# 64 bytes of padding ahead of the residual stream in SBUF: a whole network in float32 on one core

## The chip, the core and the metric

The kernel runs on one core of one Trainium2 chip. The metric is the time of one execution on the device, in microseconds (us), from the first to the last instruction with what lies around it. Less is better.

## What is computed

A batch of one, 512 tokens of width 1024, in float32, through a chain of blocks; the matrices stream in from HBM.

```python
# first block: HGRN2 mixer (8 heads, both directions, 256 context tokens), then a mixture of experts
h = modulate(x, norm1_g, sh1, sc1);   x = x + g1 * hgrn2_mixer(h, h_ctx, ...)
h2 = modulate(x, norm2_g, sh2, sc2);  x = x + g2 * moe_ffn(h2)   # 16 experts in 4 groups, top 2 of one group
x = rms_norm(x, final_g)
# second block, twice (mixer 0: differential attention + RWKV-7; mixer 1: retention)
for i in range(2):
    x = x + 0.5 * rms_norm(swiglu(rms_norm(x, g[0]), ffn_wgu[i, 0], ffn_wd[i, 0]), g[1])
    x = x + rms_norm(mixer_i(rms_norm(x, g[2])), g[3])
    x = x + 0.5 * rms_norm(swiglu(rms_norm(x, g[4]), ffn_wgu[i, 1], ffn_wd[i, 1]), g[5])
```

`swiglu(x) = (silu(x @ w_gate) * (x @ w_up)) @ w_down` has a hidden width of 2816, an expert one of 256.

## The kernel before

**Precision.** TensorE takes float32 products in a short form (`float32r`) of one pass. A value `v` is therefore kept as two tiles, `v_hi` (the short form) and `v_lo` (the rest), and a product is three matmuls into one bank: weights hi with data hi, weights hi with data lo, weights lo with data hi (`pe_products`, L353 to L355). In `matmul(out, a, b)`, `a` is the stationary operand (the weights that the array holds) and `b` is streamed; the profile writes the streamed one first, so that `bank<-mix_hi,sum_hi` streams `mix_hi` against weights in `sum_hi`. Matmuls on plain float32 tiles (transposes, small products of the mixers) take two passes.

**Weights.** A weight block is 128 x 1024 in float32, 512 KB, 4096 bytes a partition. SP issues their loads in order into a ring of four slots, `raw`; ACT copies a block into `whi` and DVE subtracts into `wlo` (L325 and L344; in the MoE stage L309 and L337). The MoE stage has a ring of eight: block `m` goes to `raw`, `whi`, `wlo` where `m % 8 < 4` and to `raw2`, `whi2`, `wlo2` else (`moe_raw`, `moe_hi`, `moe_lo`). In the profile the buffer numbers are left out, so both read `raw`, `whi`, `wlo`.

**MoE stage.** Here the weights are streamed and the tokens are stationary: per item (7 token tiles x 4 experts) 24 matmuls of 512 columns for gate and up (L2812 to L2814: `xs_hi`, `xs_lo` stationary), and 12 for down (L2840 to L2842: `at_hi`, `at_lo`). Item `i` takes blocks `6i - 2` to `6i + 1` for gate and up, so item 11 (from 685.50 us) begins with four blocks from `whi` and item 13 (from 703.52 us) has four from `whi2`. Between the first and the second block of an item lie the transposes of the item before (L2824).

**Mixer input.** The context's 256 columns, hi and lo side by side, are `hc` (`[P, 8, 512]`); `pe_block` streams them whole against `whi` (L379, L377) and their hi half against `wlo` (L380, L376).

**Seven-product passes.** Two of the three passes of an FFN's gate and up (8 pairs of blocks each) use seven half-size products in place of eight, Strassen's way. `pe_seven_pass` issues per pair the products 11, s1, 22 (of the pair before), s2, s4, 12, s3, of 12 matmuls with 256 columns each (`pe_product`, L961 to L963). Products 11 and 12 stream `h` against `whi`/`wlo`; s1 and s4 stream `h` against sums of weight blocks, `sum_hi`/`sum_lo`; 22 and s3 stream sums of `h`, `mix_hi`/`mix_lo`, against `whi`/`wlo`; s2 streams `mix` against `sum`. DVE makes the sums (L1080 to L1110), ACT their hi parts (L1024, L1033).

**Layout.** SBUF is laid out by hand, in bytes a partition. In `build`, `bump` puts a tensor at `at` and moves on by its size, rounded up to 64; `base` is the first free byte rounded up to 64, 16512 here, which is 129 x 128. In front of `x` stand `raw` to `shift2`, together 124608 bytes, an odd multiple of 64, so that `x` begins at 141120, 64 bytes past a multiple of 128. `k.low` is where `x` begins, `k.top` the end of `a32`; the stages lay their own tensors over `x` and what is behind it, from `k.low`, from `k.top` or from the place of `acc`, `sq` or `a32`: `hc`, `z_st`, `keep`, `cum` and the mixer's others (from `k.low`), `x1`, `xc1`, `whi2` (at `acc`), `raw2`, `hrow` and `wlo2` (from `k.top`), `sums`, `sum_hi`, `sum_lo`, `mix_hi`, `mix_lo` (behind half of `a32`), the retention's `r_v`, `r_qk`, `r_gate`, `r_y`, and the RWKV tensors from `rkv` (at `acc`) on. The hi and lo parts of `h` and `a`, and what is laid over them (`xs_hi`, `xs_lo`, `xrow`, `at_hi`, `ytok`, the first `held` blocks, `q_a`, `kv_a`), stand in front of `x`. All these tensors are plain rows: a tile's address in a partition is its tensor's plus a multiple of 512 bytes in the matmuls that the prediction speaks of.

Of the kernel before, what the change touches and what calls it, by code (L numbers as in the profile page):

```python
# [4783 lines left out]
def build(nc, W, vecs, small, xT, out, phases):  # L4784
    k = Kernel()
# [4 lines left out]
    with ExitStack() as ctx:  # L4790
# [10 lines left out]
        at = 0  # L4801
        def bump(name, shape, dt=F32):
            nonlocal at
            size = int(np.prod(shape[1:])) * (1 if dt == I8 else 4)
            t = sb(name, shape, dt, at=at)
            at += -(-size // 64) * 64
            return t
# [23 lines left out]
        k.shift1 = bump("shift1", [P, 2, DC])  # L4831
        k.gain2 = bump("gain2", [P, DC])
        k.shift2 = bump("shift2", [P, DC])
        k.low = at
        k.x = bump("x", [P, DC, T])
        k.acc = bump("acc", [P, DC, T])
        k.sq = bump("sq", [P, 2, T])
# [256 lines left out]
```

## Time and profile before

| | |
|---|---|
| median of three runs | 3105.99 us (3100.77 to 3107.02) |
| profiled execution: span, first to last instruction | 3101.5 us |
| profiled execution's own time | not given beside its span |
| instructions | 49298 |
| PE busy | 3016.2 us, 97%, 19037 matmuls |
| DVE busy | 2130.9 us, 69% |
| ACT busy | 1528.4 us, 49% |
| mean rate of DMA | 114 GB/s over the span |
| granted TensorE clock, mean | 0.990 |

Matmuls are pipelined: one starts before the one ahead has ended, and their ends are modelled. What a matmul takes of PE's time is therefore the distance from its start to the next one's start, which the timeline gives; the mean duration of a group is longer. The stages stand in this order: mixer input and HGRN2 mixer to about 549 us, MoE to 840, FFN to about 1300, attention and RWKV to 1700, two FFNs, retention from about 2300, and the last FFN.

### The profile page before, as it was taken

To read this page: it belongs to the slowest core of one execution; us is meant where nothing else is said; L and a number is where in the kernel's file an instruction comes from. 1 tells how busy PE (TensorE), PEld (TensorE's weight loads), DVE (VectorE), ACT (ScalarE), POOL (GpSimd) and SP (SyncE) were. 2 spreads that over 40 slices of the span, in tenths; PEclk is the share of its full clock that TensorE was granted. 3 is DMA by queue.
4 is the path that set the end of the run, shared out by engine and by line. 5 is a ranking of instruction groups with operands and counts; after the bars stand their busy time and mean duration, and the time that the engine had idled before them with its cause. 6 is when DMAs were issued, how large, how long until landed. Compare 5 with 4: busy or idle time off the path is not lost.

```text
span 3101.5 us, 49298 instructions
## 1 busy us (share of the span) xinstructions
PE 3016.2 (97%) x19037; PEld 2555.3 (82%) x19037; DVE 2130.9 (69%) x3065; ACT 1528.4 (49%) x2263; POOL 65.0 (2%) x115
## 2 busy tenths in 40 slices
PE   7999999899999999998999999999999999999997
PEld 3888887688779898667878989789988787778996
DVE  5576666899878586775468857786764443588685
ACT  4454645677745354563245535454443332455452
POOL 1000000000000000300000000000000000000000
PEclk9999999899999999999999999999999999999999
DMA  5222222799823332110023232233232222223221
GB/s 226 89 75 76 80 81 83 268 373 379 336 68 109 109 107 89 62 62 19 17 68 102 107 104 102 84 114 109 102 103 82 76 85 78 80 76 123 102 102 68
DMA packets 97101, 354.81 MB, mean 114 GB/s; under 512 B 10896, under 2 KB 11280, under 8 KB 96528
## 3 DMA queue, kind: packets, MB, share of 16 engines
q1 hardware_dynamic: 92448, 334.54, 30.5%
q0 software_dynamic: 3168, 11.54, 1.0%
q10 hardware_dynamic: 1296, 6.11, 0.5%
q8 instruction: 132, 2.16, 0.3%
q14 instruction: 57, 0.47, 0.0%
HBM read 344.27 MB, written 7.86 MB: 114 GB/s over the span
## 4 chain that ended last, share of the span: by engine, by line
PE 89%; DVE 5%; ACT 4%; issue 1%; DMA 1%; POOL 0%; SPq 0%; ACTq 0%; DVEq 0%; POOLq 0%
PE bank L353 13%; PE bank L355 13%; PE bank L354 13%; PE bank L961 7%; PE bank L963 7%; PE bank L962 7%; PE bank L2812 2%; PE bank L2814 2%; PE bank L2813 2%; PE bank L557 2%; PE bank L558 1%; PE bank L562 1%; PE cbank L379 1%; PE bank L3969 1%; PE gbank L1646 1%
## 5 line engine op out<-in xcount | busy, mean ns | idle before, releaser
L325 ACT ACTIVATE whi<-raw 128x1024 fp32r<-128x1024 f32 x310 | 319.3, 1051 | 219.1 <-PE bank L355 182.3
L344 DVE TENSOR_TENSOR wlo<-raw,whi 128x1024 fp32r<-128x1024 f32 x310 | 375.6, 1222 | 70.3 <-ACT whi L325 69.3
L353 PE MATMUL bank<-h_hi_buf,whi 128*128 128x512 f32 x1008 | 410.1, 407 | 8.1 <-DVE h_lo_buf L493 5.1
L355 PE MATMUL bank<-h_hi_buf,wlo 128*128 128x512 f32 x1008 | 394.6, 391 | 0.0
L354 PE MATMUL bank<-h_lo_buf,whi 128*128 128x512 f32 x1008 | 394.2, 391 | 0.0
L353 PE MATMUL bank<-a_hi_buf,whi 128*128 128x512 f32 x832 | 324.9, 390 | 0.5 <-DVE wlo L344 0.5
L354 PE MATMUL bank<-a_lo_buf,whi 128*128 128x512 f32 x832 | 323.7, 389 | 0.0
L355 PE MATMUL bank<-a_hi_buf,wlo 128*128 128x512 f32 x832 | 323.7, 389 | 0.0
L353 PEld LDWEIGHTS bank<-h_hi_buf,whi 128*128 128x128 f32 x1008 | 190.1, 189 | 54.6 <-DVE h_lo_buf L493 6.8
L355 PEld LDWEIGHTS bank<-h_hi_buf,wlo 128*128 128x128 f32 x1008 | 190.0, 188 | 41.3
L354 PEld LDWEIGHTS bank<-h_lo_buf,whi 128*128 128x128 f32 x1008 | 190.4, 189 | 40.2 <-issue 4.1
L337 DVE TENSOR_TENSOR wlo<-raw,whi 128x1024 fp32r<-128x1024 f32 x168 | 196.6, 1219 | 11.7 <-ACT whi L309 11.6
L353 PEld LDWEIGHTS bank<-a_hi_buf,whi 128*128 128x128 f32 x832 | 156.1, 188 | 33.5 <-DVE wlo L344 0.9
L355 PEld LDWEIGHTS bank<-a_hi_buf,wlo 128*128 128x128 f32 x832 | 156.2, 188 | 32.5
L354 PEld LDWEIGHTS bank<-a_lo_buf,whi 128*128 128x128 f32 x832 | 156.2, 188 | 32.1 <-issue 0.2
L1004 ACT ACTIVATE snap<-bank 128x256 f32<-128x256 f32 x256 | 96.6, 377 | 167.9 <-PE bank L963 167.9
L309 ACT ACTIVATE whi<-raw 128x1024 fp32r<-128x1024 f32 x168 | 168.0, 1055 | 12.9 <-DMA raw<-in_w 8.3
L1102 DVE TENSOR_TENSOR wlo<-raw,whi 128x1536 fp32r<-128x1536 f32 x64 | 112.6, 1759 | 52.3 <-ACT whi L1024 51.9
L961 PE MATMUL bank<-mix_hi,whi 128*128 128x256 f32 x512 | 144.2, 282 | 3.8 <-ACT snap L1004 3.8
L963 PE MATMUL bank<-h_hi_buf,wlo 128*128 128x256 f32 x512 | 144.6, 282 | 0.0
L961 PE MATMUL bank<-h_hi_buf,whi 128*128 128x256 f32 x512 | 144.2, 282 | 0.0
L962 PE MATMUL bank<-h_lo_buf,whi 128*128 128x256 f32 x512 | 144.0, 281 | 0.0
(724 smaller groups left out, 7229.1 us busy)
## 6 DMA issues: line engine op xcount, KB each, us to landing
raw<-in_w SPq DMA_DIRECT2D x622, 512.0 KB, 4.0
held<-in_w SPq DMA_DIRECT2D x12, 512.0 KB, 16.5
x<-in_x ACTq DMA_DIRECT2D x2, 2048.0 KB, 11.2
sorted_y<-ysb POOLq DMA_DIRECT2D x6, 512.0 KB, 7.6
token_rows<-hrow POOLq DMA_DIRECT2D x4, 512.0 KB, 4.2
out<-x SPq DMA_DIRECT2D x8, 256.0 KB, 2.0
xc<-in_xc ACTq DMA_DIRECT2D x1, 1024.0 KB, 8.7
sorted_y<-zrow POOLq DMA_DIRECT2D x1, 512.0 KB, 3.1
```

What stands on the lines that cost most here:

```text
L309: act.activation(moe_hi(k, m), moe_raw(k, m), ACT.Copy).then_inc(k.split_hi, 1)
L325: act.activation(weights(k, g)[0], k.raw[:, g.slot, :], ACT.Copy).then_inc(k.split_hi, 2 * RING + 1 if first == COND_GROUPS * RING else 1)
L337: dve.tensor_tensor(moe_lo(k, m), moe_raw(k, m), moe_hi(k, m).bitcast(F32), ALU.subtract).then_inc(k.split_lo, 1)
L344: dve.tensor_tensor(lo, k.raw[:, g.slot, :], hi.bitcast(F32), ALU.subtract).then_inc(k.split_lo, 2 * RING + 1 if first == COND_GROUPS * RI ...
L353: pe.matmul(out, w_hi, hi, start=(t == 0), stop=False)
L354: pe.matmul(out, w_hi, lo, start=False, stop=False)
L355: return pe.matmul(out, w_lo, hi, start=False, stop=(t == tiles - 1))
L961: pe.matmul(out, w_hi[:, w], m_hi, start=(fresh and t == 0), stop=False, skip_group_check=True)
L962: pe.matmul(out, w_hi[:, w], m_lo, start=False, stop=False, skip_group_check=True)
L963: last = pe.matmul(out, w_lo[:, w], m_hi, start=False, stop=(t == HALF_K - 1), skip_group_check=True)
L1004: act.activation(dst, k.bank[bank % RING][:, cols], ACT.Copy).then_inc(k.snapped, 1)
L1102: dve.tensor_tensor(pair_view(k.wlo, g)[:, T:], pair_view(k.raw, g)[:, T:], pair_view(k.whi, g)[:, T:].bitcast(F32), ALU.subtract).then_in ...
```

## The change

`k.low`, and `at` with it, is rounded up to a multiple of 128 before `x` is placed. Since `base` is a multiple of 128 too, every address from `x` on grows by 64 bytes.

```diff
         k.shift1 = bump("shift1", [P, 2, DC])
         k.gain2 = bump("gain2", [P, DC])
         k.shift2 = bump("shift2", [P, DC])
-        k.low = at
+        k.low = at = -(-at // 128) * 128
         k.x = bump("x", [P, DC, T])
         k.acc = bump("acc", [P, DC, T])
         k.sq = bump("sq", [P, 2, T])
```

| tensor | address before | after | remainder by 128 |
|---|---|---|---|
| `raw`, `whi`, `wlo` | 16512, 32896, 49280 | the same | 0 |
| `h_hi_buf`, `h_lo_buf` | 65664, 82048 | the same | 0 |
| `xs_hi`, `at_hi` | 65664, 90240 | the same | 0 |
| `a_hi_buf`, `a_lo_buf` | 98432, 114816 | the same | 0 |
| `ident` | 137856 | the same | 0 |
| `x`, `hc` | 141120 | 141184 | 64 to 0 |
| `acc`, `whi2` | 157504 | 157568 | 64 to 0 |
| `sums` | 184128 | 184192 | 64 to 0 |
| `wlo2`, `sum_hi` | 186176, 192320 | 186240, 192384 | 64 to 0 |
| `raw2`, `mix_hi` | 202560, 204608 | 202624, 204672 | 64 to 0 |
| `mat_at`, `inv`, `inv_t` | 210304, 212352, 214400 | 64 more | 0 to 64 |
| `e_neg`, `kkr`, `tmp1`, `tmp2` | 216480, 218528, 220576, 222624 | 64 more | 32 to 96 |

The instructions of every engine, their order, their waits and the transfers are the same in both kernels.

## Rows read from the trace of the kernel before

**Rows 1.** The page: busy time, share of the span, instructions; the chain by engine
```profile
PE 3016.2 (97%) x19037; PEld 2555.3 (82%) x19037; DVE 2130.9 (69%) x3065; ACT 1528.4 (49%) x2263; POOL 65.0 (2%) x115
...
PE 89%; DVE 5%; ACT 4%; issue 1%; DMA 1%; POOL 0%; SPq 0%; ACTq 0%; DVEq 0%; POOLq 0%
```

**Rows 2.** Groups by shape on DVE and ACT: count | busy us, mean ns | idle before
```profile
L1102 DVE TENSOR_TENSOR wlo<-raw,whi 128x1536 fp32r<-128x1536 f32 x64 | 112.6, 1759 | 52.3 <-ACT whi L1024 51.9
L1110 DVE TENSOR_TENSOR sum_lo<-sums,sum_hi 128x1536 fp32r<-128x1536 f32 x64 | 111.9, 1749 | 6.9 <-ACT sum_hi L1033 6.9
...
L1033 ACT ACTIVATE sum_hi<-sums 128x1536 fp32r<-128x1536 f32 x64 | 95.3, 1488 | 33.4 <-PE bank L963 33.4
L1024 ACT ACTIVATE whi<-raw 128x1536 fp32r<-128x1536 f32 x64 | 95.1, 1486 | 43.2 <-PE bank L963 43.2
```

**Rows 3.** Windows view, 1102 to 1142 us, within a seven-product pass
```profile
core 0: us, PE busy (x) PEld busy (x) DVE busy (x) ACT busy (x) POOL busy (x), PEclk, DMA share, GB/s
1102.00:1142.00 40.00, 40.00 (x343) 40.00 (x342) 35.55 (x46) 23.84 (x36) 0.00 (x0) 1.00 0.31 110
```

**Rows 4.** Timeline of PE, first matmul of each product: start us, duration us, instruction
```profile
1102.67 0.28 PE L961 MATMUL bank<-h_hi_buf,whi 128*128 128x256 f32 x1
...
1104.10 0.28 PE L961 MATMUL bank<-h_hi_buf,sum_hi 128*128 128x256 f32 x1
...
1105.45 0.28 PE L961 MATMUL bank<-mix_hi,whi 128*128 128x256 f32 x1
...
1106.87 0.28 PE L961 MATMUL bank<-mix_hi,sum_hi 128*128 128x256 f32 x1
...
1108.31 0.28 PE L961 MATMUL bank<-h_hi_buf,sum_hi 128*128 128x256 f32 x1
...
1109.73 0.28 PE L961 MATMUL bank<-h_hi_buf,whi 128*128 128x256 f32 x1
...
1111.16 0.29 PE L961 MATMUL bank<-mix_hi,whi 128*128 128x256 f32 x1
...
1112.54 0.28 PE L961 MATMUL bank<-h_hi_buf,whi 128*128 128x256 f32 x1
```

**Rows 5.** Groups by shape on PE
```profile
L353 PE MATMUL bank<-a_hi_buf,whi 128*128 128x512 f32 x832 | 324.9, 390 | 0.5 <-DVE wlo L344 0.5
...
L2812 PE MATMUL bank<-whi,xs_hi 128*128 128x512 f32 x224 | 92.5, 413 | 1.5 <-issue 1.5
...
L2840 PE MATMUL bank<-whi,at_hi 128*128 128x512 f32 x112 | 44.1, 394 | 0.0
```

**Rows 6.** Timeline of PE in the MoE stage: item 11 on `whi`, item 13 on `whi2`
```profile
687.42 0.40 PE L2813 MATMUL bank<-whi,xs_lo 128*128 128x512 f32 x1
...
689.28 0.39 PE L2812 MATMUL bank<-whi,xs_hi 128*128 128x512 f32 x1
...
690.87 0.39 PE L2813 MATMUL bank<-whi,xs_lo 128*128 128x512 f32 x1
...
705.36 0.39 PE L2813 MATMUL bank<-whi,xs_lo 128*128 128x512 f32 x1
...
709.10 0.39 PE L2814 MATMUL bank<-wlo,xs_hi 128*128 128x512 f32 x1
```

**Rows 7.** Windows view and waits of the MoE stage
```profile
549.00:830.00 281.00, 272.99 (x1279) 221.97 (x1278) 253.55 (x329) 210.55 (x275) 17.79 (x19) 0.98 0.94 353
...
ACT whi L309 <- DMA raw<-in_w: 8.3, 14, 1.8
```

**Rows 8.** Timeline of PE in the mixer's input, a block's end on `h`, then `hc`
```profile
102.12 0.39 PE L353 MATMUL bank<-h_hi_buf,whi 128*128 128x512 f32 x1
...
102.80 0.39 PE L379 MATMUL cbank<-hc,whi 128*128 128x512 f32 x1
...
103.86 0.40 PE L379 MATMUL cbank<-hc,whi 128*128 128x512 f32 x1
```

**Rows 9.** Groups by shape on PE, small float32 matmuls
```profile
L1613 PE MATMUL gbank<-qq,kk 128*128 128x128 f32 x128 | 15.6, 275 | 0.0
...
L2824 PE MATMUL cbank<-ident,a 128*128 128x128 f32 x56 | 10.7, 272 | 0.0
```

## The prediction

> **What bounds the kernel now.** I read the page's first and fourth parts first. The reader is to see one engine: PE is busy for 97% of the span, the chain that ended last lies on PE for 89% of it, and DVE and ACT together hold 9% [rows 1]. The diff adds no instruction, no wait and no transfer, and moves none; only addresses change. So time can come or go only where an instruction's duration depends on the address of its operands, and it counts where that instruction is on PE's path.
>
> The layout gives the addresses. The first buffer lies at a multiple of 128 bytes, and the sizes in front of `x` add up to an odd multiple of 64. So `raw`, `whi`, `wlo`, `h_hi_buf`, `h_lo_buf`, `a_hi_buf`, `a_lo_buf`, `rstd` and `ident` start at a multiple of 128 and stay ("even" below), and `x`, `acc`, `sq`, `sums`, `sum_hi`, `sum_lo`, `mix_hi`, `mix_lo`, `hc`, `whi2`, `wlo2` and `raw2` start 64 bytes past one ("odd") and become even. The trace of before therefore already holds both cases of nearly every operation, side by side.
>
> **DVE and ACT.** The same subtraction of 1536 elements takes 1759 ns where all three operands are even (L1102) and 1749 ns where all are odd (L1110); the same copy on ACT takes 1486 ns even (L1024) and 1488 odd (L1033) [rows 2]. The differences have no common sign and lie on engines with slack: in the tightest FFN stretch DVE is busy 35.55 of 40.00 us and ACT 23.84, while PE is busy for all 40.00 [rows 3]. I put this at nothing; PE's work hides it, and if 10 ns on each of 128 such DVE instructions did come through it would be 1.3 us.
>
> **PE in the seven-product passes of the FFNs.** These are the 5376 matmuls of 256 columns at L961 to L963: sixteen pairs of blocks in each of four FFNs, so 64 pairs of 7 products of 12 matmuls. I don't read a matmul's own duration here, since its end is modelled; I read the distance between starts. One pair runs from 1102.67 to 1112.54, 9.87 us, with no wait in it [rows 4]. Its products take, in order:
> - streamed `h`, weights `whi` (both even): 1.43, and 1.43 the second time (1109.73 to 1111.16)
> - streamed `h`, weights `sum` (even with odd): 1.35 and 1.42
> - streamed `mix`, weights `whi` (odd with even): 1.42 and 1.38
> - streamed `mix`, weights `sum` (both odd): 1.44
>
 The change makes everything even, so all seven products become alike. This is the change's main cost. If all take 1.44, a pair takes 10.08, 0.21 more, and 64 pairs 13.4 us; if all take 1.43, 10.01, 0.14 more and 9.0 us. The even ones read 1.43 today, but each of them follows an unlike product, and the one run of 12 at an unchanging distance is the 1.44; after the change no product has an unlike one ahead of it. I take +12 and keep 9.0 and 13.4 as ends. Nothing hides it: PE has no idle time there, and DVE, next in load, is at 89%.
>
> A rule of the Trainium skill speaks to this. TensorE: Matmul & The Clock Gate, section "Step-by-step: what each phase is for", says PE has two independent read ports on SBUF and that loading the next weights takes no read bandwidth from the running matmul. By that rule the seven products would take the same time and this term would be nothing; the rows above disagree by up to 0.09 us in 1.44, and I go by the rows.
>
> **PE in the MoE stage.** The counts are 3 x 224 and 3 x 112 matmuls of 512 columns (L2812 to L2814, L2840 to L2842) [rows 5]. They stream `whi`/`wlo` in four of every eight blocks and `whi2`/`wlo2` in the other four, and their weights (`xs`, `at`) are even. Half, 504, stream odd buffers. A run on `whi2` goes from 705.36 to 709.10, 16 distances of 234 ns; a run on `whi` goes from 687.42 to 690.87, 15 distances of 230 ns, of which the last seven, from 689.28, are 227 ns [rows 6]. So with 512 columns the sign is the other way: alike is the faster. The gain is between 504 x 3.7 ns = 1.9 us and 504 x 6.6 ns = 3.3 us; I take -2.2, as each item begins with small transposes after which the `whi` run needs some eight matmuls to settle. It should reach the end, since PE is busy for 272.99 of 281.00 us. But DMA is busy for 94% there, and ACT waited 8.3 us in 14 waits for a block [rows 7]; if loads follow no faster, the gain is nothing.
>
> The loads into `raw2` start 64 bytes past a multiple of 256 today and 128 past one afterwards, as those into `raw` do already, so I expect no price. The Trainium skill has a rule against the change here: DMA: Bandwidth & Descriptors, section "How a descriptor splits into AXI transactions", splits a descriptor at 256-byte boundaries and fetches whole from the boundary below its start, which for 4096 bytes makes 132 beats in place of 130. By it half the loads would be 1.5% dearer, at most 281 x 0.94 x 0.5 x 0.015 = 2.0 us, an estimate, if that page's account holds for the writing side too.
>
> **PE in the mixer's input.** `hc` (odd) is streamed against `whi` and `wlo` by 168 + 24 matmuls of 512 columns and as many of 256. Three matmuls on `h` take 0.68 (102.12 to 102.80), 0.227 each; three pairs on `hc` take 1.06 (102.80 to 103.86), 0.353 a pair [rows 8]. With like operands a pair should take 0.227 + 0.120 = 0.347, 7 ns less: 192 x 7 ns = 1.3 us. If the 256-column one went to the shortest seen, 1.35/12 = 0.113, it would be 2.5 us. I take -1.3.
>
> **The rest.** Matmuls of plain float32 on small tiles, mostly transposes, where one operand moves and the other not: L1613 (both odd) 275 ns, L2824 (even with odd) 272 ns [rows 9]. Some 400 change their relation; at 3 ns that is 1.2 us either way, and I put it at nothing. The FFN products on `h` and `a` with 512 columns touch nothing that moves (L353 on `a_hi_buf`, 832 matmuls of 390 ns) [rows 5].
>
> **Sum.** +12 - 2.2 - 1.3 = +8.5 us. The profiled execution's span is 3101.5, so 3110.0; the three runs shown have a median of 3105.99, 4.5 above that span, so I forecast **3114.5 us**. A difference of 0.2%, 6.2 us, is about what a measurement of this kernel can tell from no change; this is 0.27%. The forecast's own range: ends +9.0 and +13.4, less 5.8 at most and 0 at least, with 1.2 for the rest and some 3 us between runs: 3106 to 3121.
>
> **Rivals.**
> - *Faster.* The period is longer than 128 bytes. After the change `mix` and `sum` lie 256 bytes past a multiple of 512 against `h` and `whi`, a distance that no pair of operands has today (like ones now differ by multiples of 512). If this counts as unlike at its best, the four unlike products of a pair go from 1.35 + 1.42 + 1.42 + 1.38 = 5.57 to 4 x 1.35 = 5.40, 0.17 less, 10.9 us in 64 pairs; with 3.5 from MoE and `hc` that is 14.4, or 3091.6 us. It decides from the point where the four unlike products fall below 5.52 a pair. For it: nothing shows this distance. Against it: the two unlike relations, which differ by +192 and -192 from a multiple of 512, give the same spread (1.35 and 1.42; 1.38 and 1.42), as a period of 128 would. Chance 0.2.
> - *No change.* The spread among products comes from their order or their PSUM banks and stays: 3106. For it: `h` with `sum` takes 1.35 once and 1.42 once in the same pair, so order has a part. Against it: all alike products stand at 1.43 or 1.44. Chance 0.2.
> - *The change does not do what it says.* The blocks behind `id_st` in the RWKV mixer (`mat_at`, `inv`, `inv_t`, the second `t_rk` and `t_rb`) are even today and become odd, and some scratch tiles go from 32 to 96. All of it is in the float32 work priced above at 1.2 us, and both operands mostly move together; it lies inside the forecast.
> - *Slower loads*, the 2.0 us above with the MoE gain gone: 3106 + 12 - 1.3 + 2 = 3119. Chance 0.03.
>
> **How the numbers follow.** Forecast 0.57, faster 0.2, no change 0.2, loads 0.03. Of the forecast's cases some four in five lie over 3112.2, which with the loads gives slower 0.48; the rest of them and nearly all of no change give same 0.31; faster 0.21. The range runs from 3096 to 3120: it takes in the forecast, no change, and the upper edge of the faster case, for which a smaller effect than its full price is as likely.
>
> **What would show it.** Right: in a seven-product pass all products at 1.43 to 1.44 and a pair at 10.0 to 10.1 (a pass of eight some 1.1 to 1.7 longer than its 79.3), MoE runs on `whi2` at 227 to 230, an `hc` pair at 0.347, DVE and ACT means as before. Wrong: a pair at 9.87 or under with unlike durations still there; or PE waiting for loads in MoE.

## The result, and the profile after

The changed kernel takes 3113.15 us (median of 9 runs, 3110.64 to 3116.60); the kernel before 3105.91 us (median of 9, 3097.02 to 3107.02). The ratio is 1.0033 with a 95% interval of 1.0024 to 1.0042: slower, by a little more than the 0.2% that the prediction named as the limit of what can be told. (The two medians stand only 7.2 us apart, 1.0023: the ratio comes from all the runs and not from the two medians.) The profiled execution of the changed kernel took 3111.88 us, 1.7 over its span of 3110.2, which is 8.7 above the span of before.

The page of the changed kernel, first part (busy time of each engine, share of the span, instructions), and two of its groups:
```profile
PE 3023.5 (97%) x19037; PEld 2567.6 (83%) x19037; DVE 2129.7 (68%) x3065; ACT 1526.7 (49%) x2263; POOL 66.8 (2%) x115
...
L961 PE MATMUL bank<-mix_hi,whi 128*128 128x256 f32 x512 | 145.7, 285 | 3.8 <-ACT snap L1004 3.8
...
L961 PE MATMUL bank<-h_hi_buf,sum_hi 128*128 128x256 f32 x512 | 144.9, 283 | 0.0
```
The counts are those of [rows 1]; PE is busy 7.3 us longer and its weight loads (PEld) 12.3; DVE and ACT are not busier. The groups by shape on DVE and ACT answer to [rows 2]:
```profile
L1102 DVE TENSOR_TENSOR wlo<-raw,whi 128x1536 fp32r<-128x1536 f32 x64 | 112.5, 1758 | 61.6 <-ACT whi L1024 61.3
L1110 DVE TENSOR_TENSOR sum_lo<-sums,sum_hi 128x1536 fp32r<-128x1536 f32 x64 | 111.9, 1749 | 6.9 <-ACT sum_hi L1033 6.9
L1033 ACT ACTIVATE sum_hi<-sums 128x1536 fp32r<-128x1536 f32 x64 | 95.2, 1488 | 34.9 <-PE bank L963 34.9
L1024 ACT ACTIVATE whi<-raw 128x1536 fp32r<-128x1536 f32 x64 | 95.0, 1484 | 52.0 <-PE bank L963 52.0
```
Nothing moved but idle time: 61.6 where L1102 had 52.3, 52.0 where L1024 had 43.2. DVE and ACT wait longer for a slower PE. The 10 ns between L1102 and L1110 are still there with all operands at a multiple of 128, so they don't come from these addresses.

Timeline of PE in a seven-product pass of the changed kernel, the first matmul of each product of one pair of k-tiles, beside [rows 4] (start us, duration us, instruction):
```profile
1102.76 0.28 PE L961 MATMUL bank<-h_hi_buf,whi 128*128 128x256 f32 x1
...
1104.19 0.28 PE L961 MATMUL bank<-h_hi_buf,sum_hi 128*128 128x256 f32 x1
...
1105.63 0.28 PE L961 MATMUL bank<-mix_hi,whi 128*128 128x256 f32 x1
...
1107.08 0.28 PE L961 MATMUL bank<-mix_hi,sum_hi 128*128 128x256 f32 x1
...
1108.52 0.28 PE L961 MATMUL bank<-h_hi_buf,sum_hi 128*128 128x256 f32 x1
...
1109.95 0.28 PE L961 MATMUL bank<-h_hi_buf,whi 128*128 128x256 f32 x1
...
1111.39 0.28 PE L961 MATMUL bank<-mix_hi,whi 128*128 128x256 f32 x1
...
1112.84 0.28 PE L961 MATMUL bank<-h_hi_buf,whi 128*128 128x256 f32 x1
```
All seven products take 1.43 to 1.45 us by these rows, and the pair 10.08 in place of 9.87. The last row minus the first is 84 matmuls, 120 ns each. PE waits for nothing here, in the windows view over the same stretch as [rows 3]; the pass only gets through fewer matmuls, 336 in place of 343:
```profile
1102.00:1142.00 40.00, 40.00 (x336) 40.00 (x335) 34.68 (x45) 23.83 (x36) 0.00 (x0) 1.00 0.29 105
```
Set side by side by the same instruction, each of the eight half-width passes (the seven-product passes) ends some 1.7 us further behind; 64 pairs x 0.21 are 13.4.

The MoE stage goes the other way. Timeline of PE in item 13, a run that streams `whi2`, beside [rows 6]:
```profile
705.01 0.39 PE L2814 MATMUL bank<-wlo,xs_hi 128*128 128x512 f32 x1
...
707.73 0.39 PE L2814 MATMUL bank<-wlo,xs_hi 128*128 128x512 f32 x1
```
Twelve distances in 2.72 us are 227 ns each, where `whi2` had 234. Over the whole stage the mean distance between the starts of neighbouring matmuls (gaps over 300 ns, which are waits, left out) on `whi2` falls from 233.3 to 227.7 ns and on `whi` from 229.2 to 227.7. Windows view of the stage, the wait of ACT for a loaded block, and the group that answers to [rows 5, 7]:
```profile
549.00:830.00 281.00, 272.62 (x1294) 224.32 (x1293) 254.47 (x332) 211.86 (x278) 20.51 (x21) 0.98 0.94 356
...
ACT whi L309 <- DMA raw<-in_w: 7.3, 16, 1.6
...
L2840 PE MATMUL bank<-whi,at_hi 128*128 128x512 f32 x112 | 43.7, 390 | 0.0
```
The window holds 1294 matmuls in place of 1279, and the wait for loads did not grow (7.3 for 8.3). By the end of the stage, at 824 us, the changed kernel is 2.9 us ahead; it came into the stage 0.3 behind, and made that good before 600 us.

Where the 8.7 us between the spans lie, from the starts of the same instructions in both traces: 2.9 gained by 824 us and 0.8 given back by 894; 3.5 lost in the two passes up to 1181; 3.6 gained between 1181 and 1405; 6.8 lost up to 2286 (four passes, 4 x 1.68 = 6.7); 4.1 lost up to the end (two passes, 3.4, and 0.7 more). The 3.6 between 1181 and 1405 go with the granted clock. Windows view of the kernel before, then of the changed one, both with the clock behind POOL's column:
```profile
1243.00:1251.00 8.00, 7.44 (x16) 4.79 (x17) 3.74 (x4) 3.44 (x4) 7.67 (x5) 0.57 0.21 68
```
```profile
1243.00:1251.00 8.00, 6.03 (x24) 4.45 (x25) 5.13 (x6) 4.85 (x7) 7.72 (x5) 1.00 0.18 68
```
In the profiled execution of before, TensorE ran here mostly at the lower of its two levels (0.57 of 2.4 GHz, where the lower is 1.2) and made 16 matmuls in 7.44 us; in the one of after it kept the upper. Eight us at 0.57 are 3.4 us of work missing, an estimate; by the starts of the same instructions the kernel before lost 3.2 here. Another 1.0 went at 1363 us, where it ran 6.8 us at the lower level and the changed kernel 3.4. The kernels of the experiments have 0.63 to 1.00 in the window shown, with no order by layout that I can see, so I put this down to the execution and not to the change; a second profile of either kernel, which would show it, was not taken. Without it the spans would stand some 12 apart. The ratio of the runs, 1.0033, is 10.2 us of 3106.

### The profile page after: what moved, and what is told of

It is laid out like the page before. It is cut to its first block, busy times and chain, and to the rows that moved or that the text cites. A ratio compares the mean times of both kernels' runs of the same rounds, so it can differ in the third digit from the quotient of the medians.

```text
span 3110.2 us, 49298 instructions
## 1 busy us (share of the span) xinstructions
PE 3023.5 (97%) x19037; PEld 2567.6 (83%) x19037; DVE 2129.7 (68%) x3065; ACT 1526.7 (49%) x2263; POOL 66.8 (2%) x115
## 4 chain that ended last, share of the span: by engine, by line
PE 89%; DVE 5%; ACT 4%; issue 1%; DMA 1%; POOL 0%; SPq 0%; ACTq 0%; DVEq 0%; POOLq 0%
PE bank L353 13%; PE bank L355 13%; PE bank L354 13%; PE bank L961 7%; PE bank L963 7%; PE bank L962 7%; PE bank L2812 2%; PE bank L2814 2%; PE bank L2813 2%; PE bank L557 1%; PE bank L558 1%; PE bank L562 1%; PE cbank L379 1%; PE bank L3969 1%; PE gbank L1646 1%
## 5 line engine op out<-in xcount | busy, mean ns | idle before, releaser
L353 PE MATMUL bank<-h_hi_buf,whi 128*128 128x512 f32 x1008 | 409.9, 407 | 8.0 <-DVE h_lo_buf L493 5.1
L355 PE MATMUL bank<-h_hi_buf,wlo 128*128 128x512 f32 x1008 | 394.6, 391 | 0.0
L353 PE MATMUL bank<-a_hi_buf,whi 128*128 128x512 f32 x832 | 325.0, 391 | 0.5 <-DVE wlo L344 0.5
L355 PE MATMUL bank<-a_hi_buf,wlo 128*128 128x512 f32 x832 | 323.7, 389 | 0.0
L353 PEld LDWEIGHTS bank<-h_hi_buf,whi 128*128 128x128 f32 x1008 | 189.9, 188 | 54.7 <-DVE h_lo_buf L493 6.8
L355 PEld LDWEIGHTS bank<-h_hi_buf,wlo 128*128 128x128 f32 x1008 | 189.9, 188 | 41.0
L353 PEld LDWEIGHTS bank<-a_hi_buf,whi 128*128 128x128 f32 x832 | 156.2, 188 | 33.6 <-DVE wlo L344 0.9
L355 PEld LDWEIGHTS bank<-a_hi_buf,wlo 128*128 128x128 f32 x832 | 156.2, 188 | 32.4
L1102 DVE TENSOR_TENSOR wlo<-raw,whi 128x1536 fp32r<-128x1536 f32 x64 | 112.5, 1758 | 61.6 <-ACT whi L1024 61.3
L963 PE MATMUL bank<-h_hi_buf,sum_lo 128*128 128x256 f32 x512 | 144.9, 283 | 0.0
L961 PE MATMUL bank<-h_hi_buf,sum_hi 128*128 128x256 f32 x512 | 144.9, 283 | 0.0
```

The lines of the kernel that those rows point to most:

```text
L353: pe.matmul(out, w_hi, hi, start=(t == 0), stop=False)
L355: return pe.matmul(out, w_lo, hi, start=False, stop=(t == tiles - 1))
L961: pe.matmul(out, w_hi[:, w], m_hi, start=(fresh and t == 0), stop=False, skip_group_check=True)
L963: last = pe.matmul(out, w_lo[:, w], m_hi, start=False, stop=(t == HALF_K - 1), skip_group_check=True)
L1102: dve.tensor_tensor(pair_view(k.wlo, g)[:, T:], pair_view(k.raw, g)[:, T:], pair_view(k.whi, g)[:, T:].bitcast(F32), ALU.subtract).then_in ...
```

## The experiments

The table has, in ns, the mean time from one start to the next among the twelve matmuls of a product (11 steps), per kind of product, and for MoE the same on `whi2` with gaps over 300 ns left out. From here on "distance" is the address of the weights minus that of the streamed operand, modulo 256 bytes, and the time between two starts is the "spacing". `whi` and `wlo` lie at 128 modulo 256 in all kernels, and so do `h_hi_buf` and `h_lo_buf` in all but the last two, e8 and e9, where `h` is at 64; before, `sum` and `mix` lie at 64, after at 128.

| kernel | sum, mix at | h x whi | h x sum | mix x sum | mix x whi | MoE, on whi2 |
|---|---|---|---|---|---|---|
| before | 64, 64 | 118.9 | 115.7 | 120.0 | 117.0 | 233.3 |
| after | 128, 128 | 120.0 | 120.0 | 120.0 | 120.5 | 227.7 |
| e1 | 192, 192 | 120.0 | 116.4 | 119.3 | 118.7 | 227.9 |
| e2 | 128, 128 | 120.0 | 120.0 | 120.0 | 120.6 | 233.3 |
| e3 | 192, 192 | 120.0 | 116.4 | 119.3 | 118.7 | 229.9 |
| e4 | 96, 96 | 119.5 | 116.9 | 119.9 | 118.7 | 233.3 |
| e5 | 0, 0 | 119.4 | 118.6 | 119.0 | 119.2 | 232.9 |
| e6 | 64, 64 | 118.9 | 115.7 | 120.0 | 117.0 | 227.8 |
| e7 | 128, 64 | 119.2 | 119.1 | 113.5 | 115.7 | 227.8 |
| e8 | 128, 64; h at 64 | 117.7 | 117.7 | 117.7 | 118.1 | 229.0 |
| e9 | 128, 64; h at 64 | 117.7 | 117.7 | 117.7 | 118.1 | 227.9 |

(`mix` with `whi` reads some 0.5 high in each row: the last product of a pass has a wait inside it.)

**Take one part back, or do one part alone.** The first kernel is the changed one with the FFN's own buffers set 64 bytes on; the second is the one before with that alone.
```diff
 # e1_sums_odd_again: the changed kernel; e2_only_sums_even: the kernel before
-        at = k.arena["a32"][0] + 4 * T
+        at = k.arena["a32"][0] + 4 * T + 64
```

> The change, with sums, sum_hi, sum_lo, mix_hi and mix_lo alone moved on by 64 bytes, so that they lie 64 past a multiple of 128 again; whi2, wlo2, hc and all else stay at multiples of 128. Theory A (what counts is whether the streamed operand and the weights are alike by 128 bytes): the four unlike products of a pair come back, a pair of the seven-product pass takes 9.87 us and not 10.08, the whole falls by 64 x 0.21 = 13.4 us from the change, MoE keeps its 2.9 us, so about 3100 us, 3 to 6 under the kernel before. Rival B (the seven-product pass is longer for another reason, such as the place of x, acc or sq that ACT and DVE work on): a pair stays at 10.08 and the time at 3113.

> The kernel before, with sums, sum_hi, sum_lo, mix_hi and mix_lo alone moved on by 64 bytes to multiples of 128; x, acc, whi2, wlo2, hc stay 64 past one. Theory A: all seven products take 1.44 us, a pair 10.08, and with no gain in MoE the time is the kernel before plus 13.4, about 3119 us, the slowest of all. Rival B: as before, 3106 us, a pair 9.87.

Measured: e1 3104.08 us, ratio to before 1.0002 (0.9993 to 1.0011); e2 3117.48 us, ratio 1.0038 (1.0024 to 1.0052). So the whole loss is made by where `sum` and `mix` lie: that alone costs 0.38%, and with them 64 bytes further on the changed kernel is level with the one before. In e2 `whi2` stays at 233.3 ns as before; in e1 it is 227.9. The two parts are independent. One thing did not fit: e1 is some 4 us over its expectation of 3100. The unlike products should have gone back to their times of before, and they went only part of the way (116.4 and 118.7 for 115.7 and 117.0; a pair 9.94 us for 9.87, which is 4.7 us in 64 pairs). By a period of 128 bytes 192 is the same as 64; it isn't the same.

**Is the period 128 bytes?** Padding of 128 in front of `x` on the kernel before (a multiple of 128 changes nothing if that is the period), and padding of 32.
```diff
-        k.low = at
+        k.low = at = at + 128     # e3_pad_128
+        k.low = at = at + 32      # e4_pad_32
```

> The kernel before with 128 bytes of padding ahead of x, so that all from x on stays 64 past a multiple of 128, but goes from 320 to 448 past a multiple of 512. Theory A with a period of 128: nothing changes, the starts in a pair stand where they stood to 10 ns (9.87 us) and the time is 3106. Rival C (the period is 256 or 512 bytes): the pair or the MoE distances change, by more than 0.1 us a pair or 2 ns a matmul.

> The kernel before with 32 bytes of padding ahead of x: all from x on lies 96 past a multiple of 128. Theory A with granules of 64 bytes: 96 falls in the same half as 64, streams are unlike the weights on h and whi as before, but each row now straddles one granule more; a pair at 9.8 to 10.0 us, time 3100 to 3115. If only the remainder by 64 mattered to ACT or DVE, their 1536-element means would leave 1749 to 1759 and 1486 to 1488 ns; I expect them unchanged.

Measured: e3 3105.68 us, ratio 1.0003 (0.9994 to 1.0012); e4 3106.96 us, ratio 1.0014 (1.0005 to 1.0023). The time of e3 is that of before, but not the trace. Timeline of PE in e3, one pair:
```profile
1104.21 0.29 PE L961 MATMUL bank<-h_hi_buf,whi 128*128 128x256 f32 x1
...
1105.65 0.28 PE L961 MATMUL bank<-h_hi_buf,sum_hi 128*128 128x256 f32 x1
...
1107.07 0.28 PE L961 MATMUL bank<-mix_hi,whi 128*128 128x256 f32 x1
...
1108.49 0.28 PE L961 MATMUL bank<-mix_hi,sum_hi 128*128 128x256 f32 x1
...
1109.92 0.29 PE L961 MATMUL bank<-h_hi_buf,sum_hi 128*128 128x256 f32 x1
...
1111.30 0.28 PE L961 MATMUL bank<-h_hi_buf,whi 128*128 128x256 f32 x1
```
The product of `h` with `sum` takes 1.42 in its first place and 1.38 in its second (1109.92 to 1111.30), where before it took 1.35 and 1.42 [rows 4]; `mix` with `whi` takes 1.42 (1107.07 to 1108.49). The means of the seven products equal those of e1, which has `sum` and `mix` at the very same addresses while `x` and `whi2` lie elsewhere. So 64 and 192 are two different places and the period isn't 128. e4 came out inside its expectation: a pair takes 9.95 us, the kernel 0.14% more than before, and DVE and ACT keep their means (1758 and 1749, 1485 and 1489 ns). Its `whi2` stays at 233.3 ns, where e3's goes to 229.9.

**Distance 128, and the best of both parts.** To have room for more padding the small buffers in front of `x` are packed (`pick`, `gain2` and `shift2` into the unused ends of `tick`, `eps_col` and `eps2_col`), which brings `x` and `whi2` to 128 modulo 256. Then the FFN's buffers are put anywhere.
```diff
-        k.pick = bump("pick", [P, 2])
+        k.pick = sb("pick", [P, 2], at=arena["tick"][0] + 32)
-        k.gain2 = bump("gain2", [P, DC])
-        k.shift2 = bump("shift2", [P, DC])
+        k.gain2 = sb("gain2", [P, DC], at=arena["eps_col"][0] + 32)
+        k.shift2 = sb("shift2", [P, DC], at=arena["eps2_col"][0] + 32)
-        k.low = at
+        k.low = at = at + 128                              # e5 alone
-        at = k.arena["a32"][0] + 4 * T
+        at = k.arena["a32"][0] + 4 * T + 192               # e6 alone
+        at += 192                    # e7 alone, ahead of mix_hi
```

> The kernel before with three small tensors ahead of x (pick, gain2, shift2) moved into unused bytes of others, and padding after them, so that x and all behind it begin at a multiple of 256, 64 bytes under where they were; h, a, whi, wlo, xs stay 128 past a multiple of 256. Theory A (like or unlike by 128 bytes): the same as the change, all seven products at 1.44, a pair 10.08, MoE runs at 227, 3113 us. Theory A2, after e1 and e3 (the period is 256 bytes, since unlike at 64 and at 192 past a multiple of 256 gave a pair of 9.87 and of 9.95): a distance of 128 has not been seen in any kernel, so distances between starts differ from the change's in the pair or in MoE, by more than 0.05 us a pair or 2 ns a matmul.

> x and all behind it at 128 past a multiple of 256, as in the change (256 bytes under it, three small tensors moved to make room), but sums, sum_hi, sum_lo, mix_hi, mix_lo at the very addresses of the kernel before, 64 past a multiple of 256. Theory A2 (period 256): the seven-product pairs take 9.87 us again, MoE runs on whi2 227 ns, so the change less 13.4, about 3100 us, some 3 to 5 under the kernel before. Theory A and e1 taken at their word: 9.95 a pair, 3104. Rival B (another cause): 10.08 a pair, 3113.

> As e6, but sum_hi and sum_lo at 128 past a multiple of 256 like h and whi, and only mix_hi, mix_lo at 64 past one. If what counts is the pair of streamed operand and weights and not the place of either alone: h with sum becomes alike (1.44 us each), mix with whi and mix with sum are unlike (1.35 to 1.42): a pair 9.9 to 10.0 us, 3103 to 3110. If only the streamed operand's own place counted, h with sum would stay at 1.35 and 1.42; if only the weights' own, mix with whi would not leave 1.44.

Measured, all against the same 3102.46 us of the kernel before: e5 3109.85, ratio 1.0023 (1.0014 to 1.0033); e6 3099.45, ratio 0.9987 (0.9978 to 0.9996); e7 3099.16, ratio 0.9989 (0.9979 to 0.9998). In e5 no product has its time of the changed kernel, although every operand's address has moved by 128 against it or not at all: distance 128 is not distance 0, as e3 had shown for 64 and 192. If there is a period in powers of two, it is at least 256 bytes. The changed kernel itself shows that 256 more makes no difference there: `h` with `whi` and `h` with `sum` differ by 0 and by 256 modulo 512, and both take 120.0.

In e6, where `sum` and `mix` are at the exact addresses of before and `whi2` is like the weights, every mean of the seven products is that of before to 0.1 ns and the MoE's is that of after to 0.1: the gain of the change without its loss, as expected.

In e7 `mix` alone is 64 below. Timeline of PE, one pair:
```profile
1099.41 0.28 PE L961 MATMUL bank<-h_hi_buf,whi 128*128 128x256 f32 x1
...
1100.83 0.28 PE L961 MATMUL bank<-h_hi_buf,sum_hi 128*128 128x256 f32 x1
...
1102.27 0.29 PE L961 MATMUL bank<-mix_hi,whi 128*128 128x256 f32 x1
...
1103.65 0.28 PE L961 MATMUL bank<-mix_hi,sum_hi 128*128 128x256 f32 x1
...
1105.01 0.28 PE L961 MATMUL bank<-h_hi_buf,sum_hi 128*128 128x256 f32 x1
...
1106.43 0.28 PE L961 MATMUL bank<-h_hi_buf,whi 128*128 128x256 f32 x1
...
1107.87 0.29 PE L961 MATMUL bank<-mix_hi,whi 128*128 128x256 f32 x1
...
1109.25 0.28 PE L961 MATMUL bank<-h_hi_buf,whi 128*128 128x256 f32 x1
```
`mix` with `sum`, 1.44 in the changed kernel at distance 0, takes 1.36 at +64. Against the changed kernel `mix` has moved by 64 and all else from `x` on by 256: same order, same banks, same instructions. Like e2, that refutes the rival by which the spread comes from order or banks alone. It also meets both tests of the expectation: `h` with `sum` did not keep 1.35 and 1.42, and `mix` with `whi` left 1.44, so neither the streamed operand's place nor the weights' alone decides. The pair, 9.84, is a little under the expected 9.9 to 10.0.

But order has a part: `mix` with `whi`, also at +64, has most of its instances near 115.1 ns, not at 113.3 as `mix` with `sum` behind it. In the kernel before the order even fixes which value comes: `h` with `sum` takes 113.3 ns all 64 times behind `h` with `whi`, and 118.1 all 64 times behind `mix` with `sum`. Both write the same half of the same bank.

**All seven at the best distance.** On e7, 192 bytes of small buffers are put ahead of `h_hi_buf` and 64 behind `h_lo_buf`, so `h` lies at 64 and everything else stays. The second kernel puts the MoE's own buffers over `h` 64 bytes on, to where they were.
```diff
+        k.c_in = bump("c_in", [P, DC, 2])
+        k.c32 = bump("c32", [P, DC, 2])
+        k.gain1 = bump("gain1", [P, 2, DC])
         k.h_hi_buf = bump("h_hi_buf", [P, DC, T], F32R)
         k.h_lo_buf = bump("h_lo_buf", [P, DC, T], F32R)
+        k.shift1 = bump("shift1", [P, 2, DC])
         k.a_hi_buf = bump("a_hi_buf", [P, DC, T], F32R)
 # e9 alone: c_in and shift1 the other way round, and
-        at = k.arena["h_hi_buf"][0]
+        at = k.arena["h_hi_buf"][0] + 64     # xs_hi, xs_lo; the others over h alike
```

> The layout of e7, and h_hi/h_lo too put 64 bytes below the weights modulo 256 (192 bytes of the small buffers stand ahead of them, 64 behind; x, acc, sums, mix and the weights stay where e7 has them), so that all seven products of a half-width pass stream from 64 where the weights they load lie at 128. Theory (the distance weights minus stream modulo 256 sets the interval, +64 being the shortest at 256 columns): all seven products lock near 113.3 ns, a pair of k-tiles takes 84 x 0.1133 = 9.52 us in place of 9.86, 64 pairs: -22 us against e7. The 512-column matmuls that stream h or the copy of a token tile laid over h go from 226.7 or 227.7 to 233.3: +7.6 us for 1152 of them in the first passes of the FFNs, +4 to +5 in the MoE. Together 3086 to 3092. Rival (what helped mix/sum in e7 was where mix lies, not its distance from the sums): the products on h stay at 119 ns, only the 512-column matmuls lose, and the time is 3107 to 3113.

> As e8, with the MoE's own buffers over h (the token tiles xs and those laid beside them) put 64 bytes on, so that they lie at distance 0 from whi and whi2 again. Theory: half-width passes as e8, MoE matmuls back to 227.7 ns: 4 to 5 us below e8, 3082 to 3087. Rival of e8: 3103 to 3109.

Measured: e8 3120.58 us, ratio 1.0053 (1.0039 to 1.0067); e9 3118.10 us, ratio 1.0047 (1.0034 to 1.0061). The theory missed by 28 us and 31 us, its rival by 8 and 9; the rival's mechanism failed too, since the products on `h` left 119 for 117.7. Timeline of PE in e8, and a group of its page:
```profile
1104.35 0.28 PE L961 MATMUL bank<-h_hi_buf,whi 128*128 128x256 f32 x1
...
1105.76 0.28 PE L961 MATMUL bank<-h_hi_buf,sum_hi 128*128 128x256 f32 x1
...
1108.59 0.28 PE L961 MATMUL bank<-mix_hi,sum_hi 128*128 128x256 f32 x1
...
1110.00 0.28 PE L961 MATMUL bank<-h_hi_buf,sum_hi 128*128 128x256 f32 x1
...
1114.24 0.28 PE L961 MATMUL bank<-h_hi_buf,whi 128*128 128x256 f32 x1
...
L354 PE MATMUL bank<-h_lo_buf,whi 128*128 128x512 f32 x1008 | 399.1, 396 | 0.0
```
The pass does settle, on one value for every product, but on 1.41 us (117.7 ns) and not 1.36: a pair takes 9.89, where e7 has 9.84 (its rows above, 1099.41 to 1109.25). `mix` with `sum`, whose two operands lie where e7 has them, went from 113.5 to 117.7 though only `h` (by 192 bytes) and `a` (by 256) had moved. So one distance allows more than one spacing, and which a product takes depends on the products around it; in the passes 113.3 was seen only where products at other distances stand around it, in the kernel before at -64 too (`h` with `sum`, half of its 128 instances).

And the price was counted too low. The 512-column matmuls on `h` at L353 to L355 have a mean spacing of 227.9 ns in e7 and 233.3 in e8, while those on `a_hi_buf`, which did not move, keep 226.8. There are 3 x 1008 of them against `whi` and `wlo`, not the 1152 of my expectation (which had counted the FFNs' first passes alone), 3 x 96 more whose weights lie in `a`, and 536 in the helper with L557, L558 and L562: 3848 x 5.4 ns = 20.8 us. With 3.2 from the passes (64 pairs x 0.05) that is more than the 19 to 20 by which e8 lies over e7 (each against its own before), so a part must have fallen into waits; which part was not settled.

In the MoE the weights are `xs` and the stream `whi2`, so moving `xs` to 64 makes the distance -64 and not +64: 229.0 ns, near the 229.9 of e3, and not the 233.3 of my expectation. e9 brings it back to 227.9, at most some 1 us over the stage (1008 matmuls), and its time lies within e8's interval.

## Why the prediction was right

- **DVE and ACT at nothing:** right; 1758, 1749, 1488 and 1484 ns.
- **Seven-product passes, +12 between 9.0 and 13.4:** right, and at the upper end: 1.44 for every product, 10.08 for a pair, 13.4 in all, where the sum had +12. Of my two ends, the one read from the only run of twelve at an unchanging distance was the true one. e2 shows the term by itself: a pair at 10.08, ratio 1.0038. What the prediction gave as the reason, the weight load meeting the stream in the same half of a 128-byte line, is not right (see the period below), and no run shows what is. That page of the Trainium skill which gives the two read ports (TensorE: Matmul & The Clock Gate, "Step-by-step: what each phase is for") would have made this nothing; the runs, like the rows, disagree: the same instructions in the same order (`mix` with `sum`) take 113.5 ns in e7 and 120.0 in the changed kernel. Whether the ports have to do with it no run here shows.
- **MoE, -2.2 between 1.9 and 3.3:** right in sign and place; -2.9. It was more because runs on `whi` got faster too, 229.2 to 227.7, which I hadn't priced. That they gain because runs on `whi2` before them are now at the same distance is argued, not shown: in e4 `whi2` stays at 233.3 and `whi` still takes 228.0. Loads did not take it back (7.3 us of waiting), and nothing shows the 2.0 us that the Trainium skill's page on DMA: Bandwidth & Descriptors ("How a descriptor splits into AXI transactions") would have given by the prediction's estimate.
- **`hc`, -1.3:** wrong. This is the step that failed. I added 0.227 from runs of 512-column matmuls to 0.120 from runs of 256-column ones, and priced a pair at 0.347. Timeline of PE in the changed kernel, the same block as [rows 8]:

```profile
103.15 0.39 PE L379 MATMUL cbank<-hc,whi 128*128 128x512 f32 x1
...
103.49 0.40 PE L379 MATMUL cbank<-hc,whi 128*128 128x512 f32 x1
...
103.84 0.40 PE L379 MATMUL cbank<-hc,whi 128*128 128x512 f32 x1
...
104.20 0.40 PE L379 MATMUL cbank<-hc,whi 128*128 128x512 f32 x1
...
105.26 0.40 PE L379 MATMUL cbank<-hc,whi 128*128 128x512 f32 x1
```

The pairs take 0.34, 0.35, 0.36 and, over six, 0.352 in the mean: in the changed kernel the spacing of a run swings (227, 113, 233, 117, 241, 120, 236, 113 ns) and does not settle. From the first to the last matmul the 24 runs on `hc` take 62.07 us before and 61.91 after, 0.16 in place of 1.3. Where the two shapes alternate, a spacing measured in runs of one shape does not hold. It isn't that 0.347 can't be had: in e4, at +32, a pair takes 0.348.
- **The period:** I read the effect as two halves of a 128-byte line. e3 and e5 show that 64 and 192, and 0 and 128, differ, so that reading is wrong. It did no harm by luck: after the change all distances are 0 by either reading.
- **Overhead outside the span, 4.5 us:** this compared one execution's span with a median of others. The profiled execution of after has 1.7 outside its span. If that holds before as well, the other 2.8 is that the execution profiled before was a quick one for this kernel.
- **The number:** 3114.5 against 3113.15, and that close partly by luck. The terms as measured are 13.4 - 2.9 - 0.16 = 10.3 and not 8.5; the ratio makes it 10.2, the two medians 7.2, and the spans, without the clock's 3.6, 12.3. The cost in the passes was taken 1.4 too small, the gain in MoE 0.7 too small and the gain on `hc` 1.1 too large. What is left, some 2 us in the spans, is under "the rest" and was not traced. The prediction's inner range also has a slip: its own ends give 3105 to 3124 and not 3106 to 3121; the measured time is inside either.
- **Rivals.** *Faster* is refuted by the timeline after: `mix` and `sum` against `whi` and `h`, 256 past a multiple of 512 now, take 1.43 to 1.45. *No change* (order or banks alone) is refuted by e2 and e7, though order has a part. *Slower loads*: nothing for it.

## What to carry to other kernels

When a diff moves addresses only, look in the trace of before for the same operation at both alignments, and read the distance between starts, not the duration. Line up the streamed operand and the weights only after measuring each shape, and a sequence that mixes shapes or distances as a whole: here 512-column matmuls gained from the same move that 256-column ones lost from, and "align everything to 128" cost over four times what it gained (13.4 us against 2.9 and 0.16). Count every user of a buffer before moving it; the users outside the loop in view made most of e8's loss.

## What the runs showed that was not expected

- The spacing of float32r matmuls goes with the addresses of both operands. Sorted by the distance (weights minus stream, modulo 256 bytes), 256 columns take 120.0 ns at 0 in the changed kernel, where nothing else is near, and 118.2 to 120.0 among other distances; 113.3 to 118.1 at +64 and -64; 118.6 at 128 (e5). 512 columns take 226.7 at 0, 233.3 at +64 (e8's `h`, before's `whi2`) and at +32 (e4), 229.0 to 229.9 at -64 (e8, e3) and 232.9 at 128 (e5). So 0 is the slowest at 256 columns and the fastest at 512.
- That the distance alone counts, and not also where each operand lies, is not shown. At distance 0 `mix` with `sum` takes 120.0 with both at 64 or both at 128, 119.3 at 192 and 119.0 at 0, but its neighbours differ each time. No run moved both operands and their neighbours together by less than 256 bytes.
- The neighbours count: the same product at the same distance takes 1.35 or 1.42 us by what ran before it [rows 4], and a pass all at +64 stays at 117.7 (e8). What in the engine does this was not settled. A kernel that switches distance from product to product so as to hold 113.3 was not tried.
- The best kernels of the study, e6 and e7, are 0.13% and 0.11% faster than before, by the intervals just different from no change, and some 0.45% faster than the changed kernel (0.9987 and 0.9989 against 1.0033, each against its own runs of before).
